# Layer norms of a decoder: sums around a provisional mean inside the matmul stages, and a pass's last norm finished at the head of the next

## What is computed

```python
h = layer_norm(x, ln0_g, ln0_b)
for l in range(DEPTH):                       # DEPTH = 2
    mix = hybrid_mixer(h, ...)               # gated convolution beside gated linear attention
    h = layer_norm(ALPHA * h + mix, ln1_g[l], ln1_b[l])
    xa = memory_cross_attention(h, mem, w_xq[l], w_xkv[l], w_xo[l])
    h = layer_norm(ALPHA * h + xa, ln2_g[l], ln2_b[l])
    ff = swiglu(h, w_ffn_in[l], w_ffn_out[l])
    h = layer_norm(ALPHA * h + ff, ln3_g[l], ln3_b[l])
# layer_norm: (x - mean) / sqrt(mean((x - mean)^2) + eps) * g + b, over the 1024 features
```

## Time and profile before

| | us |
|---|---|
| median of 3 runs | 2815.52 (2814.33 to 2819.05) |
| the profiled execution, its time | 2814.45 |
| its span in the trace | 2812.7 |
| TensorE busy / VectorE / ACT / POOL | 2411.8 / 1452.5 / 710.1 / 623.1 |
| DMA, mean over the span | 280 GB/s |

### The profile page before, as it was taken

How to read it: one execution, slowest core, us unless ns; L and a number is a source line. 1 busy time by engine, 2 the same in 40 slices (tenths; PEclk the granted TensorE clock), 3 DMA queues, 4 the chain that set the end, 5 groups by cost and what they waited for, 6 DMA issues and landing times. The chain is left out here.

```text
span 2812.7 us, 24549 instructions
## 1 busy us (share of the span) xinstructions
PE 2411.8 (86%) x8322; PEld 1536.8 (55%) x8322; DVE 1452.5 (52%) x3430; ACT 710.1 (25%) x2035; POOL 623.1 (22%) x532
## 2 busy tenths in 40 slices
PE   7999999799999997988898777777788987777776
PEld 6678888676878884447443322222565443222223
DVE  3632531272335123223677777776335767777774
ACT  1321100122210002222333323332322333333333
POOL 0200000020000000000544444445003354435431
PEclk9999999999999998899999999999899999999999
DMA  6323486542237664202999999999537999999995
GB/s 248 142 98 150 179 321 241 205 179 96 96 156 306 248 241 164 90 1 90 390 421 418 422 419 412 416 422 411 229 132 285 421 421 417 418 422 411 417 418 238
DMA packets 93183, 788.24 MB, mean 280 GB/s; under 512 B 10368, under 2 KB 11648, under 8 KB 11904
## 3 DMA queue, kind: packets, MB, share of 16 engines
q0 software_dynamic: 73728, 536.90, 46.2%
q1 hardware_dynamic: 19328, 249.74, 23.1%
HBM read 785.56 MB, written 1.05 MB: 280 GB/s over the span
## 5 line engine op out<-in xcount | busy, mean ns | idle before, releaser
L1058 PE MATMUL misc<-arena 128*128 128x512 f32 x1216 | 574.6, 608 | 149.5 <-ACT arena L1118 124.5
L1179 POOL DMA_INDIRECT arena<-tables,arena x304 | 321.1, 1056 | 1078.2 <-DVE arena L979 944.1
L275 PE MATMUL tile<-xT,weight_ring 128*128 128x256 f32 x2176 | 481.4, 384 | 28.2 <-issue 13.1
L1058 PE MATMUL misc<-weight_ring,arena 128*128 128x512 f32 x832 | 394.8, 614 | 127.5 <-ACT arena L1118 101.9
L1154 DVE CUSTOM_DVE_ANT_0 arena<-arena,memT 128x1024 f32<-128x1024 f32 x304 | 372.2, 1225 | 198.9 <-DMA arena<-tables,arena 180.1
L275 PEld LDWEIGHTS tile<-xT,weight_ring 128*128 128x128 f32 x2176 | 417.3, 193 | 92.8 <-issue 32.3
L1058 PEld LDWEIGHTS misc<-arena 128*128 128x128 f32 x1216 | 219.5, 190 | 442.3 <-issue 235.7
L1179 POOL DMA_INDIRECT weight_ring<-tables,arena x208 | 259.5, 1248 | 426.1 <-DVE arena L979 363.4
L1058 PEld LDWEIGHTS misc<-weight_ring,arena 128*128 128x128 f32 x832 | 151.2, 192 | 351.8 <-issue 185.9
L1154 DVE CUSTOM_DVE_ANT_0 weight_ring<-weight_ring,memT 128x1024 f32<-128x1024 f32 x208 | 254.6, 1224 | 157.8 <-DMA weight_ring<-tables,arena 142.0
L275 PE MATMUL tile<-arena,weight_ring 128*128 128x256 f32 (+1 forms) x1112 | 270.5, 406 | 24.5 <-DVE arena L1126 10.2
(11 more groups left out here) (209 smaller groups left out, 2041.2 us busy)
## 6 DMA issues: line engine op xcount, KB each, us to landing
weight_ring<-panels SPq DMA_DIRECT2D x114, 2048.0 KB, 7.7
arena<-tables,arena POOLq DMA_INDIRECT x304
weight_ring<-tables,arena POOLq DMA_INDIRECT x208
cst<-consts SPq DMA_DIRECT2D x2, 1224.0 KB, 6.0
memT<-acts SPq DMA_DIRECT2D x2, 1024.0 KB, 17.3
arena<-c_rows SPq DMA_DIRECT2D x2, 1024.0 KB, 19.2
xT<-acts SPq DMA_DIRECT2D x1, 1024.0 KB, 4.8
arena<-acts SPq DMA_DIRECT2D x1, 1024.0 KB, 5.9
```

The costliest lines, as they stand in the source:

```text
L275: ins = nc.tensor.matmul(bank[:, 0:N], w[:, c:c + P], rhs[:, k, 0:N], start=(k == 0), stop=(k == K - 1))
L1058: ins = nc.tensor.matmul(M[2 * a + b][:, :], diag[:, s % NDIAG, :], slot(e.rows, s)[:, D + b * 512:D + (b + 1) * 512], start=first, stop=last)
L1179: pool.indirect_dma_start(slot(rows, s), None, tables, bass.IndirectOffsetOnAxis(idx[:, n % 2, k:k + 1], 0)).then_inc(landing(rows, s), 16)
```

## The change

**Norms of the loop (ln1, ln2, ln3) and ln0.** VectorE adds residual tiles 0 to 3 as they come; after the stage's tile 4 TensorE makes one ones-matmul of that sum (the provisional mean, of 512 features). VectorE subtracts it from every tile, at once for 0 to 3 and then as each comes; ACT squares. VectorE also adds the centred tiles 4 to 6 and the squares 0 to 6. After the last tile TensorE makes four ones-matmuls (two of these sums, two of tile 7 alone). The true mean differs from the provisional one by a shift; its square is taken off the mean square, and VectorE takes the shift off the tiles. The functions:

```diff
+            def four_tiles(self, w, stage, first, K, rhs, N, ready):
+                banks = {}
+                for k in range(K):
+                    ready(k)
+                    for j in range(4):
+                        if k == 0:
+                            banks[j] = self.bank(stage, first + j)
+                        c = (j * K + k) * P
+                        ins = nc.tensor.matmul(banks[j][:, 0:N], w[:, c:c + P], rhs[:, k, 0:N],
+                                               start=(k == 0), stop=(k == K - 1))
+                        if k == K - 1:
+                            self.filled(ins, stage, first + j)
...
+        centre_sum, shift_sum, square_sum = M[0][:, 0:T], M[1][:, 0:T], M[3][:, T:2 * T]
+        def centre(f):
+            nc.vector.scalar_tensor_tensor(out=xc[:, f, :], in0=centre_sum, scalar=-1.0 / (4 * P), in1=x3[:, f, :],
+                                           op0=ALU.mult, op1=ALU.add).then_inc(sem("norm_centred"), 1)
+        def half_sum_pe(pe, nth):
+            pe.wait_ge(sem("norm_half"), 3 * nth + 3)
+            nc.tensor.matmul(centre_sum, ones[:, :], rstd, start=True, stop=True).then_inc(sem("norm_centre"), 1)
+        def last_sums_pe(pe, nth):
+            pe.wait_ge(sem("norm_tail"), 2 * nth + 2)
+            nc.tensor.matmul(shift_sum, ones[:, :], sd, start=True, stop=False)
+            pe.wait_ge(sem("norm_squares"), 6 * nth + 6)
+            nc.tensor.matmul(square_sum, ones[:, :], sq[:, 0, :], start=True, stop=False)
+            pe.wait_ge(sem("norm_centred"), KD * nth + KD)
+            nc.tensor.matmul(shift_sum, ones[:, :], xc[:, KD - 1, :], start=False, stop=True
+                             ).then_inc(sem("norm_shift"), 1)
+            pe.wait_ge(sem("norm_sq"), KD * nth + KD)
+            nc.tensor.matmul(square_sum, ones[:, :], sq[:, KD - 1, :], start=False, stop=True
+                             ).then_inc(sem("norm_square"), 1)
...
+        def apply_dve(dve, nth, summed=None):
+            def shift(f):
+                nc.vector.scalar_tensor_tensor(out=xc[:, f, :], in0=shift_sum, scalar=-1.0 / D, in1=xc[:, f, :],
+                                               op0=ALU.mult, op1=ALU.add).then_inc(sem("norm_shifted"), 1)
+            dve.wait_ge(sem("norm_shift_sq"), nth + 1)
+            for f in range(2):
+                shift(f)
+            if summed is not None:
+                dve.wait_ge(sem("norm_square"), summed + 1)
+            nc.vector.scalar_tensor_tensor(out=sd, in0=square_sum, scalar=1.0 / D, in1=rstd,
+                                           op0=ALU.mult, op1=ALU.subtract).then_inc(sem("norm_variance"), 1)
+            for f in range(2, 4):
+                shift(f)
+            dve.wait_ge(sem("norm_sd"), nth + 1)
+            nc.vector.reciprocal(rstd, sd).then_inc(sem("norm_rstd"), 1)
+            dve.wait_ge(sem("norm_rstd"), nth + 1)
+            for f in range(KD):
+                if f >= 4:
+                    shift(f)
+                dve.wait_ge(sem("norm_shifted"), KD * nth + f + 1)
+                nc.vector.tensor_tensor(xc[:, f, :], xc[:, f, :], rstd, ALU.mult).then_inc(sem("norm_scaled"), 1)
```

**Where they stand.** The sums of ln0 and ln3 are made in their block; the finishing (`apply_dve`, `apply_act`) stands at the head of the next block, of each pass and of block B. The first panel of a pass is now xk 0, from memT, which needs no norm; memT is loaded once, in the prologue, which waits for it:

```diff
+                sp.dma_start(memT[:, :], acts[1]).then_inc(sem("mem_landed"), 16)
                 sp.dma_start(vb[:, :], vec_b).then_inc(sem("vec_landed"), 16)
                 first_panels(sp, 0)
+                sp.wait_ge(sem("mem_landed"), 16)
+                sp.wait_ge(sem("vec_landed"), 16)
...
-                    full_panel("glu", 0, x3)
+                    full_panel("xk", 0, mem3)
+                    e.four_tiles(e.panel("glu", 0), "glu", 0, KD, x3, T,
+                                 lambda k: pe.wait_ge(sem("norm_out"), k + 1))
                     full_panel("glu", 1, x3)
...
-                    pe.wait_ge(sem("mem_landed"), 16)
-                    full_panel("xk", 0, mem3)
...
+                    e.token_tiles(e.panel("xv", 0), "xv", 0, TT, KD, mem3)
                     pe.wait_ge(sem("att_masked"), 8)
+                    xv1 = e.panel("xv", 1)
                     norm_pe(pe, "cln", lambda f: pe.wait_ge(sem("conv_made"), f + 1), cy, CF,
-                            lambda: e.token_tiles(e.panel("xv", 0), "xv", 0, TT, KD, mem3))
+                            lambda: e.token_tiles(xv1, "xv", 2, 1, KD, mem3))
...
-                    xv1 = e.panel("xv", 1)
-                    e.token_tiles(xv1, "xv", 2, 1, KD, mem3)
+                    xk1 = e.panel("xk", 1)
+                    e.feature_tiles(xk1, "xk", 4, 1, KD, mem3, T)
                     for h in range(GH):
...
+                    e.feature_tiles(xk1[:, KD * P:], "xk", 5, 1, KD, mem3, T)
                     e.token_tiles(xv1, "xv", 2, 2, KD, mem3, start=1)
...
-                    full_panel("mix", 1, mix)
-                    xk1 = e.panel("xk", 1)
-                    norm_pe(pe, "ln1", lambda f: rd.read_wait("mix", f), x3, KD,
-                            lambda: e.feature_tiles(xk1, "xk", 4, 1, KD, mem3, T))
-                    e.feature_tiles(xk1[:, KD * P:], "xk", 5, 1, KD, mem3, T)
-                    full_panel("xq", 0, x3, lambda k: pe.wait_ge(sem("ln1_out"), k + 1))
+                    second_panel("mix", mix, 0)
+                    e.feature_tiles(xk1[:, 2 * KD * P:], "xk", 6, 2, KD, mem3, T)
+                    e.four_tiles(e.panel("xq", 0), "xq", 0, KD, x3, T,
+                                 lambda k: pe.wait_ge(sem("norm_out"), KD + k + 1))
                     full_panel("xq", 1, x3)
-                    e.feature_tiles(xk1[:, 2 * KD * P:], "xk", 6, 2, KD, mem3, T)
```

xo and fi 0 are changed as mix and xq 0 are, with no filler between the sums and fi 0. On ACT the copies of xk 6 and xk 7 stand beside ln1's affines, after the fourth and the eighth, and the kdt copy moves ahead of the Silu of the conditions:

```diff
+                    apply_act(act, 1, va, VEC_A, "ln1_g", "ln1_b", 0, lambda f: keys(6 + f // 4, 1) if f in (3, 7) else None)
```

More of the change, by code:

```diff
@@ L331, in build_program, with sqrt_table @@
+        def sqrt_table():
+            nc.scalar.activation(eps[:, 2:3], eps[:, 0:1], ACT.Sqrt)
         class Reader:
@@ L609, in _ @@
                     full_panel("xo", 0, oxx, lambda k: rd.read_wait("ox", k))
[L610 to L613 removed]
+                    second_panel("xo", oxx, 1)
+                    e.four_tiles(e.panel("fi", 0), "fi", 0, KD, x3, T,
+                                 lambda k: pe.wait_ge(sem("norm_out"), 2 * KD + k + 1))
+                    for i in range(1, 11):
+                        full_panel("fi", i, x3)
                     for i in range(KD):
@@ L627, in _, with keys, values @@
                     rd = Reader(act, A_TILES)
+                    def keys(first, count):
+                        for i in range(first, first + count):
+                            ins = nc.scalar.activation(xk[:, i, :], rd.full("xk", i)[:, 0:T], ACT.Copy)
+                            rd.free(ins, "xk", i)
+                    def values(first, count):
+                        for i in range(first, first + count):
+                            ins = nc.scalar.activation(xv[:, i % 2, (i // 2) * 512:(i // 2 + 1) * 512],
+                                                       rd.full("xv", i)[:, :], ACT.Copy)
+                            rd.free(ins, "xv", i)
+                    act.wait_ge(sem("vec_landed"), 16)
+                    apply_act(act, 0, va, VEC_A, "before_g", "before_b")
+                    keys(0, 4)
                     for i in range(CF):
@@ L849, in modulation, with residual @@
                         ins.then_inc(sem("mod_summed"), 1)
-                    def residual(stage, ln, extra=None):
+                    def residual(stage, nth, extra=None):
                         for f in range(KD):
@@ L856, in residual @@
                             rd.free(ins, stage, f)
+                            statistics_dve(dve, nth, f, lambda g: rd.read_wait(stage, g))
                             if extra and f in extra:
                                 modulation(extra[f])
-                        for f in range(KD):
-                            rd.read_wait(stage, f)
-                        norm_dve(dve, ln, x3, KD)
-                    residual("mix", "ln1")
+                    residual("mix", 0)
+                    apply_dve(dve, 1, 0)
                     modulation(0)
@@ L877, in _ @@
                         rd.free(ins, "ox", f)
-                    residual("xo", "ln2")
+                    residual("xo", 1)
+                    apply_dve(dve, 2, 1)
                     for i in range(KF):
```

164 lines of the change are left out of this document (108 added, 56 removed).

## The result

| | before | after |
|---|---|---|
| median (executions beside each other) | 2814.93 (2814.01 to 2819.05) | 2771.09 (2763.53 to 2778.92) |
| the profiled execution | 2814.45, span 2812.7 | 2777.95, span 2776.2 |

The ratio is 0.984 [0.980, 0.988]: 43.8 us less, and 14.4 less than I forecast (2785.5; range from 2778). Faster was right, the time lies outside the range. The four executions of the changed kernel are 2763.53, 2764.22, 2777.95 and 2778.92, two pairs 14 us apart, which the kernel before does not show: all its 52 executions beside this study's kernels lie between 2812.8 and 2820.7.

The account below looks back on a forecast made before the run. TensorE was taken to bound the first stages (busy 502 of 525 us), with gains only where it idles or sums norms. Terms summed to 30.0 us, from 2814.45 to 2784.5; with 1.07 for the median, forecast 2785.5, range 2778 to 2796.

Parts of the forecast that it names:

- Bound and prologue: TensorE chain bounds the passes; prologue's first matmul at 19.1 us instead of 25.31, gain 6.2, with SyncE's panels last.
- ln2: Norm before fi: first matmul 7.03 us after T (TensorE's turn from the stage's last tile), was 11.94; gain 7.6 for two.
- ln1: Norm before xq: scores at T+37.9, with a new 1.36 us wait for xk 7's bank; gain 7.7 for two.
- Mix: Mix stage after the RMS sums: more matmuls in between end the wait for gated tiles; gain 2.3 for two.
- kd, qe, ke: Moved from POOL to DVE: 1.4 us gained by the kdt copy, 0.8 lost to a 0.4 wait before xv 1.
- Turn: Loop turn between passes: first matmul at T+14.05 instead of T+21.52, running xk 0, which needs no norm; gain 7.0.
- the first rival: At the loop turn, TensorE's extra 3.7 us start delay goes; time 2781.8 us; chance 0.08.
- Block B: Second pass to the MLA stage: nothing covers the norm's chain, first matmul T+19.5 instead of T+18.56; loss 0.95, plus 0.43.
- New waits: Rival: DVE late at the masks and panels queued behind xk 7 cost 2 + 3 us per pass; 2795.5; chance 0.09.
- No cover: Rival: four_tiles waits on the finished norm despite xk 0; turn and prologue give back up to 13 us; 2798.5; chance 0.03.
- k-major: Rival: six panels changing bank at each matmul cost 0.16 us a record; time 2847 us; chance 0.02.
- The sum of the first part: All terms from the prologue to the MLA stage together, a gain of 30.0 us.

Follow-up runs that it names:

- e11: Changed kernel with glu 0, xq 0 and fi 0 run tile by tile instead of four tiles side by side; 2762.69 us, ratio 0.9807.
- e12: Changed kernel with kd, qe and ke put back on POOL; median 2792.08 us, ratio 0.9911.
- e13: Changed kernel run a third time, nothing edited but a comment; median 2766.26 us, ratio 0.983.
- e1: Changed kernel run again, nothing edited but a comment; median 2765.48 us, ratio 0.9814.
- e9: Kernel before the change plus ten idle VectorE copies at the head of the MLA (latent attention) stage; median 2800.07 us, ratio 0.9941.
- e7: Changed kernel plus four idle VectorE copies at the head of the MLA stage; median 2774.34 us, ratio 0.9859.
- e8: Changed kernel plus eight idle VectorE copies at the head of the MLA stage; median 2764.71 us, ratio 0.9837.
- e10: Changed kernel with one panel loaded ahead at a block end instead of two, plus three idle copies; median 2765.97 us, ratio 0.9821.
- e15: Changed kernel with one panel ahead instead of two, panels behind norms tile by tile, and ten idle copies; median 2761.88 us, ratio 0.9796.
- e2: Changed kernel with one panel loaded ahead at a block end instead of two; median 2766.34 us, ratio 0.9825.
- e3: Changed kernel with ln0 and ln3 finished in the block that sums them, xk 0 still first; median 2786.49 us, ratio 0.9898.

## Why the prediction was right, and where it failed

**Bound and prologue: right.** First matmul 19.13 for 19.1; SyncE was the last to arrive, 9.7 us behind its panels and 0.2 behind the others.

**ln2: right.** T+6.90 for 7.03, in both passes (780.82 to 787.72 in the second). The records behind it were slow as priced: 15.51 us for 64 where the glu panel takes 13.98, 1.5 more, in pass 1, and about 3 in pass 2; I had 2.5. The clock fell and rose as windows of the changed kernel show:
```profile
282.34:284.34 2.00, 2.00 (x5) 1.64 (x6) 1.93 (x6) 1.98 (x5) 0.00 (x0) 0.50 0.12 49
284.34:286.34 2.00, 2.00 (x9) 1.69 (x8) 1.37 (x4) 1.62 (x3) 0.00 (x0) 0.76 0.00 0
286.34:288.34 2.00, 2.00 (x11) 1.77 (x10) 0.00 (x0) 1.36 (x2) 0.00 (x0) 1.00 0.00 0
```
The prediction set beside this term a rule of the Trainium skill ("TensorE: Matmul & The Clock Gate", Part 1), that the slow matmuls differ between runs, and said it would scatter the term by about a microsecond; the two passes are apart by 1.6 us, somewhat more. I didn't ask what the same scatter does to a stage with many short idle times.

**ln1: right.** T+37.74 for 37.9. The new wait before xk 7's bank is there, 0.81 for 1.36, between the 6th and 7th record of xq (201.22); e11 takes it away.

**Mix: right.** The gated tiles are no longer waited for: 161.87 to 189.92 is 28.05 with the extra matmul's 0.43, so 27.6, the warm time of 128 records.

**kd, qe, ke: half right.** The copy's wait went, but the wait of 0.4 before xv 1 did not come (111.85 to 125.69 is 13.84, the warm time). The larger error is of accounting: I took the move as worth 1.4 us. With xk 0 gone from behind r, POOL's 17.3 us would have stood on TensorE's path, and e12 shows that this move keeps 29.7 us. It is what allows the new first panel.

**Turn: right.** T+13.96 for 14.05. TensorE's start came 3.75 after POOL's (522.43 to 526.18), 3.7 before, so the first rival falls. In the prologue it is absent (19.03 to 19.13), as in the kernel before. What it is was not tested.

**Block B: right.** -0.50 for -0.95 from T, with the head now bare.

**The other rivals.** New waits: 0.81 us a pass, nothing of the 5. No cover: glu follows xk 0 without a bracket (34.66). k-major: 64 records in 13.98 us beside 27.79 for 128 tile by tile (e11), no difference.

**The sum of the first part** was 30.0 and came out at 34.2 in this pair (33.6 to 35.8 with the MLA starts of e13 and e1). Of the 4.2 above, 1.6 and 2.1 lie in the passes; the xk 0 panel's slow clock, the missing wait of 0.4 and the clock in other stages are of this size. I have not resolved them further. This alone would have given 2781, inside the range.

**The step that failed** is the last sentence of the sum: "What follows the loop [...] isn't touched and moves as a block". The rest does: 1516.3 to 1519.8 us in all 17 profiles. The attention doesn't: 205, 216.5 or 221.5 us, by how long the clock is still at the 1.2 GHz level when it begins. The kernel before had the long one in each of its executions, as far as their times tell; the changed one has the short one in nine of thirteen, again by their times. So of the gain between the medians over 13 executions (49 us), 34 belong to the code that was changed and about 15 to the clock of a stage that it moved. The prediction put nothing at this place, and no rival named it. The second part is not the change's merit: ten idle copies give it to the old kernel too (e9).

What stays open: how a microsecond or two more of slow clock at the stage's start lead to 27 us of it some 96 us later, and what sets the rise, 22.4 or 23.9 us behind T in profiles of one kernel. The order by the rise was found in the traces afterwards and no kernel was aimed by it; my aims by the span's time missed in e7, e8, e10 and mostly in e15.

## What to carry to other kernels

- Before a gain or loss of under one per cent is credited to an edit, cut both profiles at the end of the edited part and compare the untouched stages. If one of them changed its length, read its granted clock: here 13.5 us of e2 did not show in its median at all, and the 7.3 us of e3 showed as 20.7. Delaying the untouched stage by a microsecond or two of idle work, in the old kernel, tests it directly. Count the stage's start from the clock's rise, not from the span's beginning.
- A norm between matmul stages costs what TensorE idles: bring the sums into the stage before, put a stage that needs no norm behind the block end, and look which engine held the operand of the next one. That last step was the dearest (e12).
- At a barrier ask which transfer the waiting queue really needs. One panel fewer was worth 11 us at the three block ends of e2.

## What the runs showed that I had not expected

- One stage of 675 matmul records with short waits took 205.0, 216.5 or 221.5 us at a granted clock of 0.98, 0.91 or 0.89, in the same program, and the clock's rise, 2.9 to 5.6 us behind its first matmul, goes with the length in all 17 profiles. The Trainium skill says of the gate, "TensorE: Matmul & The Clock Gate", Part 1, that its ramp costs less than one per cent of a typical kernel's span, and that one shouldn't fit to a particular count of slow matmuls. 16 of 2800 us is 0.6 per cent, so the trace agrees on the size; but the kernel before lost them in every execution, by its times, and that is systematic when two kernels are compared.
- A TENSOR_TENSOR of 128x512 on POOL took 17.27 us while VectorE ran its convolution (busy 16.15 of 17.24 us), and the two behind it, with VectorE idle, 1.26 each (e12).
- On VectorE a TENSOR_SCALAR copy of 128x256 in fp32 repeats every 0.21 us, where the norm's additions repeat every 0.34.
